# Six input tiles of the first attention's output projection multiplied inside its loop, with logits on three banks

## What is computed

```python
logits = jnp.einsum('bqhd,bqkhd->bhqk', qb, ks) * HEAD_DIM ** -0.5
p = jax.nn.softmax(logits, axis=-1)
o = jnp.einsum('bhqk,bqkhd->bqhd', p, vs)      # per head
return (o * jax.nn.silu(g)) @ w_out            # the output projection, 1024 x 1024
```

## Time and profile before

| | us |
|---|---|
| median of 3 runs | 991.11 |
| lowest and highest run | 990.96, 991.43 |
| profiled execution, first to last instruction | 989.2 |
| first attention's loop on PE, up to the first product of `oa` | 125.4 to 146.2 |

### The profile page before, as it was taken

The page is one execution under the profiler, slowest core; times in us unless marked ns, Lnnn a source line. Parts: engine busy times, 40 slices in busy tenths (PEclk is TensorE's granted clock), DMA queues, the critical chain, the costliest instruction groups (busy, mean ns, idle before and its releaser), DMA issues.

```text
span 989.2 us, 16695 instructions
## 1 busy us (share of the span) xinstructions
PE 972.1 (98%) x6532; PEld 879.3 (89%) x6532; DVE 686.6 (69%) x1056; ACT 556.1 (56%) x856; POOL 209.3 (21%) x199
## 2 busy tenths in 40 slices
PE   9999989999999999999999999999999999999997
PEld 8779759989988988798899899999898989989985
DVE  5789785854666687665556779776687665767973
ACT  5556673665765474555355466555445555546662
POOL 0002034300344440012003005221044301202610
PEclk9999999999999999999999999999999999999999
DMA  9634425465334447246414655457546432555441
GB/s 363 241 132 166 175 87 208 162 221 214 128 128 141 174 133 271 108 171 213 150 64 170 213 186 187 181 194 281 186 170 255 163 135 93 198 183 181 172 152 43
DMA packets 24831, 172.93 MB, mean 175 GB/s; under 512 B 2752, under 2 KB 2880, under 8 KB 4416
## 3 DMA queue, kind: packets, MB, share of 16 engines
q1 hardware_dynamic: 23040, 160.66, 45.6%
q10 hardware_dynamic: 1728, 11.40, 3.0%
HBM read 166.81 MB, written 5.24 MB: 174 GB/s over the span
## 4 chain that ended last, share of the span: by engine, by line
PE 93%; DVE 2%; ACT 2%; DMA 1%; issue 1%; POOL 0%; SPq 0%; ACTq 0%; DVEq 0%
PE banks L506 38%; PE banks L594 16%; PE banks L512 14%; PE banks L514 7%; PE banks L504 6%; PE banks L656 4%; PE banks L710 1%; DMA raw<-w 1%; PE banks L761 1%; PE banks L762 1%; DVE work L1725 1%; PE banks L743 1%; PE banks L917 1%; PE banks L834 0%; DVE work L1737 0%
## 5 line engine op out<-in xcount | busy, mean ns | idle before, releaser
L1598 DVE TENSOR_TENSOR wl<-raw,wh 128x1024 fp32r<-128x1024 f32 x300 | 379.7, 1275 | 157.4 <-ACT wh L1090 156.0
L1090 ACT ACTIVATE wh<-raw 128x1024 fp32r<-128x1024 f32 x300 | 313.2, 1054 | 180.6 <-PE banks L506 76.1
L512 PE MATMUL banks<-xx,wh 128*128 128x512 f32 x544 | 192.5, 398 | 0.0
L506 PE MATMUL banks<-xx,wh 128*128 128x256 f32 x1024 | 190.3, 284 | 0.0
L506 PE MATMUL banks<-yy,wh 128*128 128x256 f32 x1024 | 187.8, 285 | 0.1
L506 PEld LDWEIGHTS banks<-xx,wh 128*128 128x128 f32 x1024 | 161.4, 192 | 1.4 <-issue 0.5
L506 PEld LDWEIGHTS banks<-yy,wh 128*128 128x128 f32 x1024 | 160.4, 192 | 0.7 <-issue 0.5
L514 PE MATMUL banks<-xx,wl 128*128 128x256 f32 x544 | 151.8, 279 | 0.0
L506 PE MATMUL banks<-xx,wl 128*128 128x256 f32 x512 | 144.8, 283 | 0.0
L506 PE MATMUL banks<-yy,wl 128*128 128x256 f32 x512 | 138.6, 283 | 0.0
L512 PEld LDWEIGHTS banks<-xx,wh 128*128 128x128 f32 x544 | 102.0, 187 | 22.7
(11 more groups left out here) (221 smaller groups left out, 1449.3 us busy)
## 6 DMA issues: line engine op xcount, KB each, us to landing
raw<-w SPq DMA_DIRECT2D x149, 1024.0 KB, 4.8
m_scratch<-yy ACTq DMA_DIRECT2D x2, 1024.0 KB, 5.9
k_scratch<-kt ACTq DMA_DIRECT2D x2, 1024.0 KB, 8.2
kt<-k_scratch ACTq DMA_DIRECT2D x2, 1024.0 KB, 5.8
yy<-m_scratch ACTq DMA_DIRECT2D x2, 1024.0 KB, 6.0
raw<-w SPq DMA_DIRECT2D x2, 512.0 KB, 5.2
h<-xt SPq DMA_DIRECT2D x2, 512.0 KB, 6.1
v<-memt ACTq DMA_DIRECT2D x1, 1024.0 KB, 7.7
```

Of the source, the lines that this page charges most:

```text
L506: return pe.matmul(b[:, j, :], weights, o_[:, kk, :], start=k0 + k == 0 and q == 0 and (j == 0 or not both_open), stop=k0 + k == KT * p.de ...
L512: pe.matmul(b[:, j, :], wh[:, slot, j, k * P:k * P + P], operand[:, :, tile0 + k0 + k, :], start=k0 + k == 0, stop=False, skip_group_check ...
L1090: act.activation(wh[:, n % 2, j, :], raw[:, n % RAW_SLOTS, j, :], ACT.Copy).then_inc(hi_ready, 1)
L1598: dve.tensor_tensor(wl[:, n % 2, j, :], raw[:, n % RAW_SLOTS, j, :], wh[:, n % 2, j, :].bitcast(F32), ALU.subtract).then_inc(lo_ready, 1)
```

## The change

A new function on PE, `first_tiles`, issues the three products of one input tile and one half of `oa`'s first chunk. The loop of `attA` calls it at the head of steps 9 to 20: tile 0 half 0 in step 9, tile 0 half 1 in step 10, and so on to tile 5 half 1 in step 20. With half 0 it first waits for `y_hi` and `g_lo` of the tile. `project("oa", ..., done=6)` then has only tiles 6 and 7 of that chunk left, for each half in turn, and its two rounds are written out where a loop of the sequencer stood. Since bank 0 is now in use during the loop, the logits of heads 6 to 15 rotate over banks 4, 5 and 1, and `score_pair` waits, for every pair from heads 6 and 7 on, until DVE has read the logits of all heads before the pair.

```diff
+        OA_FROM, OA_TILES = 9, 6
...
-                if a >= 8 and a % 4 < 2:
-                    return bank[PH["va"].pair + a % 2]
+                if a >= 6:
+                    return (bank[4], bank[5], bank[PH["va"].pair + 1])[a % 3]
...
+            def first_tiles(name, operand, ready, tiles, halves=(0, 1)):
                 p = PH[name]
                 oh, ol = [operand[:, q, :, :] for q in range(2)]
-                enter(p)
+                slot, b = p.n0 % 2, b3(p.pair)
+                for k in tiles:
+                    for j in halves:
+                        if k == 0:
+                            pe.wait_ge(lo_ready, 2 * p.n0 + j + 1)
+                        if j == 0:
+                            for which in ready(k):
+                                pe.wait_ge(*which)
+                        for q in range(3):
+                            mm = pe.matmul(b[:, j, :], (wh, wl, wh)[q][:, slot, j, k * P:k * P + P], (oh, oh, ol)[q][:, k, :],
+                                           start=k == 0 and q == 0 and j == 0, stop=k == KT - 1 and q == 2,
+                                           skip_group_check=True)
+                        if k == KT - 1:
+                            mm.then_inc(w_used, 1)
+
+            def project(name, operand, ready=None, hooks={}, tile0=0, done=0):
...
+                if not done:
+                    enter(p)
...
-                            for tiles in (range(KT - 2), range(KT - 2, KT)):
+                            for tiles in ((range(done, KT),) if done else (range(KT - 2), range(KT - 2, KT))):
...
+                elif done:
+                    round_(0, True)
+                    round_(1, False, {}, None)
...
-                if heads[0] >= 10 or heads[0] == 4:
+                if heads[0] == 8:
+                    pe.wait_ge(act_evac, PH["va"].end)
+                if heads[0] == 4:
                     pe.wait_ge(s_read, 2 * (u - 3))
-                elif heads[0] == 6:
+                elif heads[0] >= 6:
                     pe.wait_ge(s_read, 2 * (u - 1))
-                elif heads[0] == 8:
-                    pe.wait_ge(act_evac, PH["va"].end)
...
+                        if t >= OA_FROM and (t - OA_FROM) // 2 < OA_TILES:
+                            if t == OA_FROM:
+                                pe.wait_ge(act_evac, PH["va"].end)
+                            first_tiles("oa", yy, y_ready("A", g_lo, GBASE["A"], 1), [(t - OA_FROM) // 2], [(t - OA_FROM) % 2])
...
-            project("oa", yy, y_ready("A", g_lo, GBASE["A"], 1))
+            project("oa", yy, y_ready("A", g_lo, GBASE["A"], 1), done=OA_TILES)
```

More of the change, by code:

```diff
@@ L466, in enter @@
                     pe.wait_ge(evac[p.before.reader], p.before.end)
-            def project(name, operand, ready=None, hooks={}, tile0=0):
+            def first_tiles(name, operand, ready, tiles, halves=(0, 1)):
                 p = PH[name]
                 oh, ol = [operand[:, q, :, :] for q in range(2)]
-                enter(p)
+                slot, b = p.n0 % 2, b3(p.pair)
[13 more added lines that the diff above has]
+            def project(name, operand, ready=None, hooks={}, tile0=0, done=0):
+                p = PH[name]
+                oh, ol = [operand[:, q, :, :] for q in range(2)]
+                if not done:
+                    enter(p)
                 per = 2 * p.deep
```

## The result

The changed kernel takes 993.48 us (median of 17 runs, 991.84 to 994.59) against 991.18 us before (17 runs beside it, 990.92 to 991.50): a ratio of 1.0023, 95% interval 1.0016 to 1.0029, so 2.3 us slower. The runs of before lie within 0.6 us. Those of after come in two groups: three at 991.84, 991.98 and 992.08, and fourteen from 993.04 up, with no run between. The mean granted clock is 0.998 in the three and 0.995 to 0.997 in the fourteen. The profiled execution is one of the fourteen (993.21 us, span 991.3).

A forecast was written before the change was run, and what follows sets the result against it. It took VectorE to set the loop's pace, with 0.48 us per two steps spare on TensorE. 2.3 us late minus 1.39 back gave +0.9: profile 990.1, plus 0.0019 ms to the median, 992.0 us; range 990.2 to 994.4.

The forecast's parts named there:

- the rival of the falling clock: TensorE's clock halves in the quiet stretch before tile 7 arrives: up to 1.9 us lost, 993.9 us; chance 23 in 100.
- The likeliest case: Loop 2.3 us late, 1.39 us back behind it, clock kept: 992.0 us, range 991.3 to 993.1; 60 in 100.
- a granted clock of 0.50 near 152: Sign of being wrong: TensorE at half clock around the wait for tile 7, before the second chunk.
- The loop: Twelve added groups in steps 9 to 20 make the last value product 2.3 us late, 147.6 instead of 145.29.
- An entry: Extra time in the loop when TensorE enters a group of this kind of product: 0.11 us, bounds 0 and 0.18.
- The last logits: After five groups in steps 9 to 13, TensorE's last logits come 0.9 us late, bounds 0.36 and 1.26.
- The low part of tile 4: POOL's input to the group ahead of step 17's turn, taken with gated tile 4 as 0.45 us late (0.1, 0.9).
- The group of tile 4: Stands ahead of step 17's turn and waits for POOL; TensorE goes on at 144.22, nothing covering what follows.
- The stricter wait: `score_pair` waiting for VectorE to have read earlier heads' logits: at most 0.1 us, covered by later lateness.
- Tile 7: Behind the loop, 0.89 us from last value product to gating, then 3.5 us through VectorE and POOL (4.07 before).
- my lower bound: Time from tile 7's gating to its low part if POOL is not hindered at all: 1.7 us.
- The sum: 2.3 us late in the loop, 1.39 us back behind it: +0.9 us, from +0.2 to +2.2.

The follow-up runs named there:

- the filled kernel: The changed kernel with 10 and 7 idle products ahead of TensorE's waits for tile 7's high and low parts; 991.93 us, ratio 1.0006.
- four tiles in order: The changed kernel with four tiles in the loop instead of six and the remaining products in the order of their inputs; 990.04 us, ratio 0.9988.
- with four tiles: The changed kernel with four tiles in the loop instead of six, steps 9 to 16; 992.96 us, ratio 1.0016.

## Why the prediction was right and wrong

The number, 992.0 us, was 1.5 us too low, inside its range, which reached that high only for the rival of the falling clock. The likeliest case came in no more than 3 runs of 17 (991.84 to 992.08) and in the filled kernel (991.93); in the other 14 that rival came. So in its mechanism the prediction failed by its own words: it fails "if the clock falls in most executions", and one of its signs of being wrong, a granted clock of 0.50 near 152, is there. It also called the change no change within 2 us; the 2.3 us measured (interval 1.6 to 2.9) lie beside that line, on the slower side.

- **The loop, right within its bounds.** An entry costs 136.28 - 136.06 - 0.12 = 0.10 us behind the products of an attention; I took 0.11. The last logits start at 138.62; before the change, one beat behind the earlier trace rows, they started at 134.98 + 3.16 = 138.14. That is 0.48 late, or 0.62 counted from the first turn, where I had 0.9. The low part of tile 4 starts at 142.98 instead of 142.86, 0.12 late or 0.26 by that count, where I had 0.45. The group of tile 4 waits for POOL in front of the turn, as forecast, and goes on at 143.97 (144.22). From there to the last value product it is 3.24 us (3.40). Together that product starts at 147.21 instead of 147.6. The stricter wait, which I took at no more than 0.1 us, costs 0.16 at one pair (0.64 instead of 0.48 in the kernel with the banks alone) and is part of this lateness.
- **Tile 7, right.** 0.95 us to the gating (0.89), then 151.63 - 148.16 = 3.47 us (3.5). Of the two waits for POOL the first was the longer, 1.51 against 1.04, where I had the longer one last. That VectorE's `lo` is the cause is shown by the kernel that holds it back: 150.19 - 148.49 = 1.70, from its gating at 148.49 to 149.46 + 0.73, which was my lower bound. By the Trainium skill, "SBUF — State Buffer", section "Who interferes with whom", a VectorE instruction with two SBUF inputs contends with a GpSimd instruction that reads SBUF, and the order of issue decides which of them blocks. The trace agrees: `lo` starts at 148.50, POOL's cast 0.15 us later, and the cast takes 1.32 us beside `lo`, 0.40 without.
- **The sum, right with the clock kept.** Seven products at 0.12 behind 151.68 would put the second chunk at 152.52, 0.55 later than before, or 0.69 counted from the first turn; the filled kernel measures 0.70 more; I had 0.9. The sum's bounds were 0.2 and 2.2.
- **The step that failed: "Chance 23 in 100" for the falling clock.** I put two things against the fall: that in the earlier trace rows no product came at all, while here five would, and that waits of 0.67 us in the loop left the clock alone. Neither protects. Five products, 0.93 us of work in 3.43, did not keep the clock in 14 of 17 executions, and 0.67 us amid a busy loop says nothing of 1.51 and 1.04 us one behind the other. Its price was rightly sized: the low level lasts 3.4 us (I took 3.7 from the warm-up), and the fourteen runs, median 993.50, lie 1.52 above the three, median 991.98 (up to 1.9).
- By the rule of the Trainium skill, "TensorE: Matmul & The Clock Gate", Part 1, an idle TensorE is put back to half its clock, and I had weighed that against these rows. The windows agree in part: the clock is 0.50 from 152.10 to 155.50, behind a stretch in which TensorE was mostly but not wholly idle, 0.93 us of work in 3.43 with no single wait above 1.51.

What stays open: why the same program falls in 14 executions and not in 3. The profile is of one execution, and the others are told apart by their time and mean clock alone. Four runs at 994.23 to 994.59 with a mean clock of 0.995 and 0.996 hint at a longer or a second fall; no trace shows it.

## What to carry to other kernels

Work that looks movable on a busy engine may be the cover of another engine's chain: before moving it, time the latest input behind it without it, and put the products that remain in the order in which their inputs come. Where the cover goes, the hole costs more than its length, since TensorE's clock can fall behind it: here a change that cost 0.7 us with the clock kept cost 2.3 in most runs. Times that fall into two groups, one with a lower mean clock, are the sign to look for, and idle products in the hole are the test.

## What the runs showed of the hardware

By the times of the runs, the clock at its full level outlived waits of 0.58 and 0.19 us in all 11 (`lo` held back), and waits of 0.18 and 0.93 among 3.3 us of products in all 11 (four tiles in order). With 1.03 and 0.92 us, little between them, the slower group had 4 runs of 11; with 1.51 and 1.04 it had 14 of 17. So the same instructions have no single time near such a place. In both falls that a trace shows, the granted clock was 0.50 in the stretch behind the waits (152.10 to 155.50, and 150.90 to 154.20 with four tiles) although TensorE was busy throughout it.

Two operations of POOL that met two of VectorE's 128x1024 subtractions took 1.32 and 1.58 us instead of 0.40 and 0.73, while the two subtractions took 2.55 us, hardly more than two free ones (2 x 1.23).
